# Two halves per weight block, a reordered start and a later pooling branch in a one-core transformer kernel

## What is computed

```python
mod = silu(c) @ ada_w + ada_b                    # 12 groups of 512 columns for each layer
h   = rms_norm(x, norm_mix) * (1 + scale) + shift  # shift: groups 0, 1; scale: groups 2, 3
p, q, k, v = split(h @ w_in)                     # p: 256 pooling channels, GQA heads for q, k, v
pool = (window_means(p) - p) @ pool_w            # windows of 2, 4, 8 and 16 tokens
x = x + gate * (concat(pool-branch, attention(rope(q), rope(k), v)) @ w_out)
```

## Time and profile before

| | us |
|---|---|
| median of 3 runs (2538.51 to 2540.66) | 2540.08 |
| the profiled execution | 2537.89 |
| its span, first to last instruction | 2536.1 |
| PE busy in it | 2442.1 (96%) |
| first unit starts | 56.28 |
| first matmul of layer 0's attention | 214.22 |

### The profile page before, as it was taken

How to read it: one execution, slowest core, us unless ns; L and a number is a source line. 1 busy time by engine, 2 the same in 40 slices (tenths; PEclk the granted TensorE clock), 3 DMA queues, 4 the chain that set the end, 5 groups by cost and what they waited for, 6 DMA issues and landing times.

```text
span 2536.1 us, 34037 instructions
## 1 busy us (share of the span) xinstructions
PE 2442.1 (96%) x13345; PEld 1915.0 (76%) x13345; DVE 996.0 (39%) x1426; ACT 851.0 (34%) x1382; POOL 772.9 (30%) x413
## 2 busy tenths in 40 slices
PE   6998999999999999999899999999999998999998
PEld 3676667788888888688577768888887656888887
DVE  4356651411122112544456332221527665523322
ACT  3224652322122122332556332222423564322321
POOL 1161001223232323231011234444543531444443
PEclk8999999999999999999999999999999998999999
DMA  7540006521222223422020243333333200333332
GB/s 262 166 108 26 1 1 214 168 67 58 67 58 66 62 61 94 127 67 52 7 43 10 59 133 100 96 94 100 91 100 83 81 1 26 92 98 93 100 98 76
DMA packets 335970, 209.76 MB, mean 83 GB/s; under 512 B 29299, under 2 KB 308444, under 8 KB 335842
## 3 DMA queue, kind: packets, MB, share of 16 engines
q1 hardware_dynamic: 332880, 201.89, 27.2%
q10 hardware_dynamic: 2898, 6.05, 0.7%
q0 software_dynamic: 64, 0.04, 0.0%
HBM read 205.82 MB, written 2.12 MB: 82 GB/s over the span
## 4 chain that ended last, share of the span: by engine, by line
PE 84%; issue 5%; DVE 5%; DMA 2%; ACT 2%; POOL 2%; SPq 0%; DVEq 0%; ACTq 0%; POOLq 0%
PE G L1579 21%; PE G L1580 21%; PE G L1581 21%; PE G L1775 5%; PE G L1803 4%; PE G L1788 4%; DMA raw<-in_l_ada_w_dram 2%; POOL wlo L898 2%; PE G L1650 1%; PE G L1746 1%; PE G L1617 1%; PE G L1821 1%; PE G L1601 1%; DVE ssq L2046 1%; PE G L1602 1%
## 5 line engine op out<-in xcount | busy, mean ns | idle before, releaser
L898 POOL TENSOR_TENSOR wlo<-raw,whi 128x1024 fp32r<-128x1024 f32 x282 | 680.1, 2412 | 1528.8 <-ACT whi L1084 1528.7
L1579 PE MATMUL G<-big_a,whi 128*128 128x512 f32 x2016 | 743.7, 369 | 8.5 <-POOL wlo L898 4.9
L1580 PE MATMUL G<-big_a,wlo 128*128 128x512 f32 x2016 | 729.3, 362 | 0.0
L1084 ACT ACTIVATE whi<-raw 128x1024 fp32r<-128x1024 f32 x282 | 298.9, 1060 | 1275.7 <-PE G L1581 1127.5
L1581 PE MATMUL G<-big_a,whi 128*128 128x512 f32 x2016 | 726.0, 360 | 0.0
L1579 PEld LDWEIGHTS G<-big_a,whi 128*128 128x128 f32 x2016 | 380.9, 189 | 86.5 <-issue 15.1
L1580 PEld LDWEIGHTS G<-big_a,wlo 128*128 128x128 f32 x2016 | 380.7, 189 | 63.8 <-issue 7.0
L1581 PEld LDWEIGHTS G<-big_a,whi 128*128 128x128 f32 x2016 | 379.5, 188 | 60.5
L1579 PE MATMUL G<-big_b,whi 128*128 128x512 f32 x856 | 315.7, 369 | 3.2 <-POOL wlo L898 2.3
L1580 PE MATMUL G<-big_b,wlo 128*128 128x512 f32 x856 | 315.6, 369 | 0.0
L1581 PE MATMUL G<-big_b,whi 128*128 128x512 f32 x856 | 314.3, 367 | 0.0
(11 more groups left out here) (245 smaller groups left out, 2277.7 us busy)
## 6 DMA issues: line engine op xcount, KB each, us to landing
raw<-in_l_ada_w_dram SPq DMA_DIRECT2D x96, 512.0 KB, 5.0
raw<-in_l_ffn_w_gate_dram SPq DMA_DIRECT2D x44, 512.0 KB, 3.8
raw<-in_l_ffn_w_up_dram SPq DMA_DIRECT2D x44, 512.0 KB, 3.8
raw<-in_l_ffn_w_down_dram SPq DMA_DIRECT2D x32, 512.0 KB, 4.0
raw<-in_w_up_dram SPq DMA_DIRECT2D x32, 512.0 KB, 4.0
raw<-in_w_down_dram SPq DMA_DIRECT2D x32, 512.0 KB, 3.7
raw<-in_w_in_dram SPq DMA_DIRECT2D x28, 512.0 KB, 3.8
raw<-in_l_w_in_dram SPq DMA_DIRECT2D x24, 512.0 KB, 3.9
```

The costliest lines, as they stand in the source:

```text
L898: pool.tensor_tensor(wlo[:, u % 2], raw[:, r % RING], whi[:, u % 2].bitcast(F32), ALU.subtract).then_inc(raw_free[r % RING], 1)
L1084: act.activation(whi[:, u % 2], raw[:, r % RING], ACT.Copy).then_inc(hi_done, 1)
L1579: pe.matmul(o, whi[:, u % 2, k], rlo[:, k, t0:t0 + w], start=k == 0, stop=False)
L1580: pe.matmul(o, wlo[:, u % 2, k], rhi[:, k, t0:t0 + w], start=False, stop=False)
```

## The change

The diff has four parts.

**The start.** Groups 1, 2 and 3 no longer go through the ring: SP loads them into parts of the two large buffers (`staged`), and PE reads them there (`ada_staged`). The 24 small vectors move from ACT's to SP's queue, between groups 1 and 2; the rope and pooling tables and the pooling weights move behind the first norm. x is squared by token rows before it is transposed, with the sum in the same instruction; half the xT copies move from DVE to ACT. The spread root is multiplied into `xn` by DVE; the gain and the shift are applied afterwards by ACT (`hhi`) and DVE (`tmp`), four tiles as soon as group 2 is known, the other four after group 3, whose product and turn stand inside `first_units`.

**The order of units.** k (0, 1), q (2 to 7), v (8, 9), pooling (10, 11). Groups 4 to 9 follow units 2 to 7. The loads of units 0 to 3 stand together ahead of group 4.

**The pooling.** POOL does the windows after it has lowered the first two blocks of `wout`; PE's pooling product and its two scalings on ACT and DVE move behind the attention. The first unit of each `wout` square multiplies k-tiles 2 to 7 first, then 0 and 1; the wait for `pooldone` stands behind it as planned (`between={7: ...}`), ahead of tiles 0 and 1.

**Halves.** ACT and POOL split each block as two instructions of 128x512; `lo_half` counts first halves, `raw_free` second halves. PE starts a unit on `lo_half` and waits for `raw_free` ahead of its fifth k-tile. This is in all 282 units.

```diff
-        for i in range(4):
-            plan_ada(0, i)
-            plan_aux(("adaT", 0, i - 1) if i else "vec")
-            for m in XIN_AFTER[i]:
-                plan_aux(("xin", m))
-        plan_aux(("adaT", 0, 3))
+        plan_ada(0, 0)
+        for m in range(4):
+            plan_aux(("xin", m))
+        for i in (1, 2):
+            for q in range(4):
+                plan["ada", 0, i, q] = (None, None, cnt["g"])
+            cnt["g"] += 1
+            if i == 1:
+                for m in range(4, KD):
+                    plan_aux(("xin", m))
+                plan_aux(("spread", 0))
+                plan_aux("vec")
+                plan_aux(("adaT", 0, 0))
+        plan_aux(("adaT", 0, 1))
+        plan_aux(("adaT", 0, 2))
...
-        S0, L0_Q, L0_POOL, L0_V = {}, range(4, 10), (2, 3), (10, 11)
+        S0, L0_Q, L0_V, L0_POOL = {}, range(2, 8), (8, 9), (10, 11)
...
-        ADA_IN0 = [(0, 4 + i) for i in range(6)]
+        LAST_GAIN = (0, 3)
+        ADA_IN0 = [LAST_GAIN, None] + [(0, 4 + i) for i in range(6)]
...
-                pool.wait_ge(hi_done, u + 1 + 4 * j)
-                pool.tensor_tensor(wlo[:, u % 2], raw[:, r % RING], whi[:, u % 2].bitcast(F32),
-                                   ALU.subtract).then_inc(raw_free[r % RING], 1)
+                for half, k in enumerate((0, 4)):
+                    pool.wait_ge(hi_done, 2 * u + half + 1 + 8 * j)
+                    ins = pool.tensor_tensor(wlo[:, u % 2, k:k + 4], raw[:, r % RING, k:k + 4],
+                                             whi[:, u % 2, k:k + 4].bitcast(F32), ALU.subtract)
+                    ins.then_inc(raw_free[r % RING] if half else lo_half, 1)
...
-                act.activation(whi[:, u % 2], raw[:, r % RING], ACT.Copy).then_inc(hi_done, 1)
+                for k in (0, 4):
+                    act.activation(whi[:, u % 2, k:k + 4], raw[:, r % RING, k:k + 4], ACT.Copy).then_inc(hi_done, 1)
...
+            for t in range(6):
+                if t == 4:
+                    act.wait_ge(*when(("set", "cload"), 16))
+                ins = act.activation(bf[:, D * t:D * t + D], xtok[:, t, :], ACT.Square, accum_out=stat[:, 2, t:t + 1])
...
-                pe.wait_ge(raw_free[r % RING], r // RING + 1 + j)
+                pe.wait_ge(lo_half, u + 1 + 4 * j)
...
+                    if max(order[0:at + 1]) >= 4 and (at == 0 or max(order[0:at]) < 4):
+                        pe.wait_ge(raw_free[r % RING], r // RING + 1 + j)
...
+            for m in range(KD):
+                if m >= 4:
+                    dve.wait_ge(*when(("set", "xact"), m - 3))
+                dve.tensor_tensor(xn[:, m, :], xT[:, m, :], ps(key), ALU.mult).then_inc(PH["set", "xnorm"], 1)
...
+            first_gain(2)
+            first_norm(0)
+            first_gain(3)
+            first_norm(4)
```

More of the change, by code:

```diff
@@ new lines, in _ @@
+            act.wait_ge(*when(("set", "rest"), 1))
+            act.activation(rsb[:, 1, 0:6], stat[:, 2, 0:6], ACT.Sqrt, bias=eps[:, 0:1],
+                           scale=1.0 / D).then_inc(PH["norm0", "std"], 1)
+            ada(0, 0)
+            ada(0, 1)
+            for m in range(4, KD):
+                key = ("xin", m)
+                act.wait_ge(*auxiliary(key))
+                release(act.activation(xT[:, m, :], ps(key), ACT.Copy), key)
+                act.wait_ge(gfree[group_of(key) % 4], group_of(key) // 4 + 1)
+                act.sem_inc(PH["set", "xact"], 1)
@@ new lines, in _, with first_norm @@
+            act.wait_ge(*auxiliary("vec"))
+            act.dma_start(halves[0:12], A["mats"][0:12, 6]).then_inc(PH["set", "halves"], 16)
+            ada(0, 2)
+            upper(0)
+            upper(1)
+            def first_norm(k):
+                act.wait_ge(*when(("set", "xnorm"), k + 1))
+                for q, (t0, w) in enumerate(X_CTX):
+                    ins = act.activation(hhi[:, k, t0:t0 + w], xn[:, k, t0:t0 + w], ACT.Identity,
+                                         bias=mod[:, 0, k, q:q + 1], scale=amix[:, 0, k, q:q + 1])
+                ins.then_inc(PH["norm0", "hi"], 1)
@@ L1442, in _ @@
+            act.wait_ge(*when(("set", "gain"), 1))
+            for k in range(4):
+                first_norm(k)
+            ada(*LAST_GAIN)
+            act.wait_ge(*when(("set", "gain"), 2))
+            for k in range(4, KD):
+                first_norm(k)
             with nc.allow_non_contiguous_dma(reason="small vectors"):
-                def rows_of(name, width=P):
-                    return A[name].rearrange("(a p) -> a p", p=width)
-                two = lambda name, w: A[name].rearrange("a (b p) -> (a b) p", p=w)
@@ new lines, in _ @@
+            ada(0, 0)
+            pe.wait_ge(*when(("set", "xload"), 16))
+            pe.wait_ge(*when(("set", "cload"), 16))
+            for m in range(4):
+                turn_tokens(m)
+            ada_staged(1)
+            for m in range(4, KD):
+                turn_tokens(m)
+            a, g = plan["spread", 0]
+            pe.wait_ge(*when(("set", "ones"), 16))
+            pe.wait_ge(*when(("norm0", "diag"), 1))
+            take_group(g)
+            for t0, w in X_CTX:
+                mm = pe.matmul(G[g % 4][:, t0:t0 + w], ones_d, rsb[:, 0, t0:t0 + w], start=True, stop=True)
```

318 lines of the change are left out of this document (184 added, 134 removed).

## The result

The changed kernel takes 2499.18 us (median of 4 runs, 2495.44 to 2500.76) where the kernel before took 2540.37 beside it (2538.51 to 2540.7). The ratio is 0.9837, with a 95% interval of 0.982 to 0.9854. Two later comparisons on other chips gave 0.984 (0.9827 to 0.9853) and 0.9839 (0.982 to 0.9858). The profiled execution took 2495.44, with a span of 2493.6.

The account below looks back on a forecast made before the run. PE was taken as the bound, 96% busy, leaving only the start and seams between stages to gain. Terms 23 + 2 - 1 + 4.5 = 28.5 us took the median from 2540.08 to 2511.6, range 2503 to 2522.

Parts of the forecast that it names:

- Part 2: Gap at 76 us behind the first two units: third unit starts at 69.2, last unit of the stage ends at 189.8.
- Part 1: Kernel start: first unit at 43.5 us, 12.8 earlier; first two units end at 67.6 against 75.82, 8.2 earlier.
- rival 2: Gap behind the first two units returns because group 4 waits for ring slots; at worst 9.1 us lost, 2520.7; chance 0.08.
- Part 3: End of input stage: attention starts at 190.9 against 214.22, 23 us earlier; clock gives 2 more, moved pooling product costs 1.
- the 0.7 to 3.4: Cost in us of the pooling product placed between the attention and the first output unit; taken as 1.
- Part 4: Halves, in all units: PE's waits for the low part shrink by 5.8 us, later second halves cost some; net 4.5.
- The five waits: PE's waits for wlo outside the input stage, each at a stage's third unit: 7.2 us in all, 5.8 removable.
- Rival 1: Start gives only part: 25 handovers each 0.2 longer, 5 us, and half clock 2 more; 2518.6; chance 0.17.
- Rival 3: Second wait in each unit costs PE time in loops; at 0.13 us per unit the kernel takes 2548; chance 0.03.
- Rival 4: Group 3 inside the first two units stalls PE, losing all 12.8 us saved at the start; 2524.4; chance 0.04.
- the better case: Better than forecast by a faster gain part and a full clock, down to 2503 us; chance 0.06.

Follow-up runs that it names:

- parts 1 to 3: The changed kernel with whole blocks again (no halves; start, unit order and pooling as changed): 2515.25 us, ratio 0.9903 to the kernel before; mean of three ratios 0.9897.
- one place less: The changed kernel with groups 4 to 9 following units 1 to 6 instead of 2 to 7: 2507.75 us, ratio 0.9868 to the kernel before.
- POOL's instruction in two: Whole-block version of the changed kernel with only POOL's low part cut in two, PE waiting for all of it: 2515.88 us, against 2513.72 uncut.
- the filled waits: Whole-block version of the changed kernel, PE filling its wait in three third units with overwritten matmuls: 2510.82 us, against 2513.52 unfilled.
- the halves alone: The kernel before with only the two halves per block put in: 2527.51 us against 2538.44, ratio 0.9957.
- quarters: The changed kernel with blocks split in four instructions on ACT and POOL, PE waiting for each part: 2494.99 us; repeated 2496.31 against 2500.65.

## Why the prediction was wrong

The direction and the order of the parts held. The sum was too small by 12.7 us, and the halves' term carries most of it.

**The division.** Part 2 counted the third unit 1.6 us behind the second, with half blocks. Undivided, this wait is 1.87 us where the changed kernel has 0.37. So of the 28.5 forecast, 6.1 belonged to the halves (4.5 and this 1.6) and 22.4 to parts 1 to 3. Measured are 14.8 and 26.2: the halves were short by 8.7, the rest by 3.8.

**Part 1: right in its chain, 1.9 us long.** The squares took from 13.57 to 19.92, 6.35 and not 7.5, as squares follow each other by 1.04: the accumulator read of 0.19 overlaps the squares on both sides of it. Products began at 27.93 (forecast 29.8) and took 7.00 (7.7), at a spacing of 0.875 and not at the 0.95 of one. The two turns were slow, as I took them. The gain part took 0.87 where I took 1.14. The first unit was forecast at 43.5 and came at 41.64, 0.8 below my 42.4 to 44.3. The Trainium skill's rule on one source in SBUF ("VectorE: DVE Perf Modes", section "Mode 2×_2P — use both read ports for one tensor") gives a rate, and the forecast's estimate from it alone was half the row, 0.57 for this tile. The trace agrees with the rate per element, and not with the estimate for the tile: in this kernel the 512 and the 256 columns take 543 and 407 ns, 136 for 256 columns, where the form with PSUM took 747 and 475, or 272. A fixed part of some 270 ns for each instruction is left. The wait in the two units was 0.76 at 55.64, forecast 0.8; they ended at 64.12 (67.6), as there was no second wait and the clock was 0.92 rather than 0.86.

**Part 2: right.** The third unit started 1.83 behind the second's end (1.6), and PE's first 118.55 us there had no idle time; I had 120.6, of which 1.0 was the idle time of before, which did not come back. The ring's next slots, rival 2, were in time; with one place less they are not (5.20 us of wait).

**Part 3: right.** The attention began 1.11 behind the last unit (1.1) and 28.6 earlier than before (23.3), all of the difference from parts 1 and 2. The clock over its first 7.8 us was 1.00 in this trace and 0.78 in the other two. The pooling product took 4.54, most of it at half clock, and the price fits the 0.7 to 3.4: the first output unit started 29.4 earlier instead of 28.6, and without a wait.

**Part 4: the step that failed.** "The five waits are 0.8, 0.3, 2.3, 1.5 and 2.3, and with at most 1.6 off each this is 5.8." The waits did fall so: 7.2 us to 1.6 outside the stage, 5.6 of 5.8. Wrong was to take the waits for the low part as all there is, and with it the sentence "In all other units the split ends long before use, and it costs nothing." The term stood at 4.5 us and measured 14.8, or 8.7 more than it and its share of part 2 together. What the runs show in its place, from the means of three traces of parts 1 to 3 and three of the changed kernel, by the start or end of stretches of units:

| place | parts 1 to 3 | changed | ahead by |
|---|---|---|---|
| last input unit of layer 0 ends | 186.90 | 184.95 | 1.95 |
| third feed-forward unit, layer 0, starts | 465.97 | 464.62 | 1.35 |
| layer 1's input stage, fourth unit, starts | 1045.81 | 1043.31 | 2.50 |
| output product, layer 1, starts | 1387.27 | 1383.82 | 3.45 |
| output product, layer 1, ends | 1436.75 | 1430.33 | 6.42 |
| third feed-forward unit, layer 1, starts | 1464.44 | 1455.61 | 8.83 |
| that stretch of units ends | 1823.64 | 1812.21 | 11.43 |
| output product, layer 2, starts | 2102.50 | 2089.62 | 12.88 |
| its stretch ends | 2160.48 | 2144.48 | 16.00 |
| last unit ends | 2503.02 | 2487.02 | 16.00 |

Of these 16.0 us, 7.1 are waits for the low part (9.1 to 2.0, the one of the first stage among them). 3.0 are waits for DVE (24.7 to 21.7), whose instructions no longer stand behind POOL's long ones (with the reserve of the section on POOL's instruction in two). Some 2.9 are matmuls at half clock behind the third units' waits: 1.4 at the layer 1 output product in each of three traces of parts 1 to 3 and in none of the changed kernel, 1.4 at the feed-forward stage in one of three, and about 1.4 at the layer 2 output product in two of three. Together 13.0. Some of the remaining 3 us lies in delays too short for the list of waits, which begins at 0.15 us. From the third feed-forward unit of layer 1 the first 1400 matmuls take 317.5 us in every trace whose clock stays up, and the 169 behind them 41.2 to 41.3 us in all five traces with whole blocks (the kernel before, parts 1 to 3, the filled waits) and 39.1 in the changed kernel and in the halves alone. Of these 2.1 us the list shows 0.85 for DVE and 0.18 at a start that the changed kernel does not have; most of the rest are starts late by under 0.15 us, two of them on the low part itself, and the matmul behind each late start, which follows by 0.34 us and not 0.23. What is then left, under 2 us, I cannot place; the attention alone moves by 2 us from run to run.

The kernel before shows it too. Its timeline at the third feed-forward unit of layer 1, and the window behind it, then the same two of the changed kernel, where this unit starts with no wait and the clock stays at 1.00:

```profile
1488.21 0.50 PE L1579 MATMUL G<-big_a,whi 128*128 128x512 f32 x1 [1.50 <-POOL wlo L898]
...
1489.25 0.63 PE L1579 MATMUL G<-big_a,whi 128*128 128x512 f32 x1
```
```profile
1488.20:1498.00 9.80, 9.79 (x36) 7.93 (x37) 2.67 (x2) 2.45 (x4) 3.56 (x2) 0.83 0.37 109
```
```profile
1454.29 0.50 PE L1638 MATMUL G<-big_a,whi 128*128 128x512 f32 x1
1454.62 0.40 PE L1639 MATMUL G<-big_a,wlo 128*128 128x512 f32 x1
```
```profile
1454.20:1464.00 9.80, 9.80 (x44) 8.04 (x44) 1.70 (x3) 4.30 (x8) 6.82 (x6) 1.00 0.38 109
```

The forecast read the length of the five waits and not the window behind any of them. I also set 1.3 us against the halves, for nine groups that might wait for the later end of the second part (0.1 to 0.2 each); this cost nothing that a trace shows.

**The rivals.** Rival 1 went the other way: the handovers of the new chain were no longer than the sum. Rival 2 did not occur, and its mechanism is real. Rival 3 did not occur: with two waits in each of 282 units the stretches in the loops are no longer than before (465.97 to 966.03 in parts 1 to 3 and 464.62 to 964.65 in the changed kernel, 500.06 and 500.03 us). Rival 4 came to 0.76 us at one place. The measured time lies beyond the better case, which I gave 0.06 and bounded at 2503. Both of its terms came (the gain part 0.27 faster, the clock at 1.00 in one trace of three), but they are not what carried the time there. It lacked a term for what lies behind a wait.

## What to carry to other kernels

Price a wait of TensorE by what lies behind it as well: look at the granted clock of the window that follows, since here 2.3 us of waiting cost about another 1.5 in five of eight cases, and 1.2 us another 1.6 in two of two; the length of a wait did not tell which. And price the length of an instruction by whom it holds up on a shared resource, then ask whether they are on the path: here POOL's halves alone made DVE's two-input instructions about twice as fast, and the time did not move, as PE paid for them at the low part. When the order of loads on one queue is in question, ask which of them is needed first, and not which is large.

## What the runs showed that I had not expected

VectorE's instructions with two inputs in SBUF take as long as POOL's instruction beside them leaves: the gate product's 128x512 form 2276 ns at POOL's 2412, 1180 with POOL's instruction in two, and 696 in the changed kernel, where 691 is the shortest of the 44 of that line. Shorter instructions on POOL do not shorten them all alike: the 128x768 form went from 2139 to 1031 with POOL's instruction in two but only to 1821 in the changed kernel, and in quarters the 128x512 form is back at 1101. It goes by where POOL's instructions start beside them, not by their length alone. The one-input form with both sides in SBUF is held too: 1.77 us beside POOL and 0.86 without. The Trainium skill ("SBUF — State Buffer", section "SBUF: two separate sides") has the two engines share one pair of ports that is locked for a whole instruction; the trace agrees, in both forms.

The same kernel on another chip moved by up to 1.3 thousandths in its ratio (0.9868 and 0.9881), 3 us, so a split of a few us between two causes needed both kernels on one chip, and the trace of the place.
